# A Mamba-2 and gated DeltaNet block: state-space output by channels in the chunk loop, and a chunk-by-chunk layout for broadcast rows

## Chip, cores and metric

The kernel runs on one core of one Trainium2 chip. The metric is the device time of one execution in microseconds (us); the figure shown for a kernel is the median over its runs.

## What is computed

One layer over a sequence of 1024 tokens of width 1024, in float32: a state-space (SSD) branch and a gated DeltaNet branch in parallel, merged by gates, then a gated conv-MLP and a per-layer embedding. The change touches the state-space recurrence only. With heads `h` of dimension `p` (16 heads of 64 channels), two groups of 8 heads, state size `n` = 128:

```python
seg = a_cum[..., :, None] - a_cum[..., None, :]
lmat = jnp.exp(jnp.where(causal, seg, -jnp.inf))
scores = jnp.einsum('bclgn,bcsgn->bcgls', cc, bc)
y_diag = jnp.einsum('bcgrls,bcsgrp->bclgrp', scores[:, :, :, None] * lmat, xc)
...
y_off = jnp.einsum('bclgn,bcgrpn,bcgrl->bclgrp', cc, prev, jnp.exp(a_cum))
return (y_diag + y_off)          # then + D * x, * silu(z), a norm by group
```

## The kernel before

All five engines run programs written out by hand, each with its own order of work; semaphores tie them together. `after(engine, sem, n)` makes an engine wait until `sem` has been raised n times since the start. DMAs are issued from SP's queue (nearly all loads) and ACT's queue (stores of finished tiles); within a queue a wait holds back all that stands behind it.

The parts, in order of time:

- The head: normalised input, transposed; then tiles of the input projection with their convolutions. On the way ACT (`head_exps`) makes the exponentials of the decay sums and stores the cumulated decay rows of all heads to HBM as `cum_rows` [128 rows, 1024 tokens]. DVE waits for that store (`cum_kept`) ahead of its `raw_op` L3284.
- Pairs of projection tiles by seven products each (L615), with ring buffers `ring_a` that go to the spill area by stores on ACT's queue. A ring slot is rewritten (L624) once its last store has landed.
- Stage A, 8 chunks of 128 tokens: norms and Gram matrices of the DeltaNet branch, set between the k-steps of 16 plain projection tiles (L498, L501, L502). SP loads per chunk `dec_a` twice from `cum_rows` (L1628: 8 rows of 128 tokens, the same rows to all 128 partitions) and `qkv_a` (L1634).
- The chunk loop (`sp_mixer`, `pool_mixer`, `pe_mixer`, `act_mixer`, `dve_mixer`), 8 chunks of 128 tokens, both branches. Between its parts PE runs `gemm(steps[i])`: k-steps of further projection tiles, 12 steps in each of the first four chunks and 8 in the others.
- The rest: branch outputs, MLP, embedding; not touched.

PE's order in a chunk `c` is: products with the DeltaNet state (`ks`, `qs`); `off` (L1128: for each of two groups the C rows of the tokens are stationary and 512 state columns move, so the result has tokens on partitions); gemm; `vn` (needs DVE's `rhs`, L1351); `diag(c, 0)` (L1107), gemm, `diag(c, 1)`; `ds`, `o`; gemm; `st` (L1151); the next chunk's `invert_r`; eight transposes of `ysum` (L1158); gemm; the next chunk's `x_rows_of`, `invert_h`, `scores`; gemm; sums of squares (L1173, needs ACT's L1254 and DVE's `xc`, L1311); `invert_h` (L1088), gemm, `invert_h`; transposes of the DeltaNet output (L1183, need DVE's L1392); gemm.

`diag` takes one head's decay-weighted scores `dec[:, h, :]` as the stationary operand and a pair of heads of `xc` as the moving one, so half of each 128 x 128 result is the wrong head's and DVE (`add_diag`) picks the other half. An f32 matmul shows as two matmul instructions in the trace.

DVE in a chunk: `rhs` (L1348, L1351), `qs` (L1356), `ysum` = off product times exp of the decay sums (L1360), two `add_diag` (L1340), state and output sums, `yssm` += transposed `ysum` (L1383), `yssm` *= `zt` (L1386), next chunk's `xc` (L1311) and inverses, L1392, L1398, L1401, and the scores times decays for the next chunk (`mix_scores`, L1334).

POOL in a chunk: scaling of the states (L1017, L1020), the skip term (L1010), one weight split (L483, L485), then the next chunk's `decays` on `dec` [128 x 2048] (L994, L996), which wait for the load of `dec` (`load_dec`, L923: 16 rows of `cum_rows`, 128 tokens each, to all partitions), and `xcd` (L1003). ACT then takes the exponential (L1237) and, where one is due, empties a projection tile (`mg_evict`, L1219); PE can't begin the next projection tile before that.

SP's order in the loop is `load_g(c)`, `load_qk`, `load_xbc`, `load_bv` for c + 1, a block of weights, then `load_dec`, `load_kd`, `load_mq`, `load_z` for c + 1, then `load_inv(c + 2)`. `load_dec` of the next chunk waits for both `diag` parts of this one.

Of the kernel before, what the change touches and what calls it, by code (L numbers as in the profile page):

```python
# [7 lines left out]
D_MODEL, SEQ = 1024, 1024  # L8
P = 128
# [26 lines left out]
def hybrid_block_kernel(nc, x, p, g_mix_pre, w_in, conv_ssm_w, conv_ssm_b, ssm_dt_bias, ssm_a_log, ssm_d, ssm_norm_g,  # L36
# [7 lines left out]
    def scratch(name, shape):  # L44
        return nc.dram_tensor(name, shape, f32).ap()
# [6 lines left out]
    cum_rows = scratch("cum_rows", [P, SEQ])  # L52
# [12 lines left out]
    def sem(name):  # L65
        return ctx.enter_context(nc.semaphore(name))
# [12 lines left out]
    at = 0  # L79
# [200 lines left out]
    def weights_k(w):  # L280
# [44 lines left out]
    in_xbc, in_qk, in_bv, in_kd, in_mq, in_dec, in_z, in_g, in_nt, in_d = (  # L325
        sem(n) for n in ("in_xbc", "in_qk", "in_bv", "in_kd", "in_mq", "in_dec", "in_z", "in_g", "in_nt", "in_d"))
# [5 lines left out]
    r_done, h_done, xt_done, sc_done, ks_done, qs_done, off_done, vn_done, ds_done, o_done, diag_done, st_done, yt_done, \  # L332
        yssq_done, ot_done = (
            sem(n) for n in ("r_done", "h_done", "xt_done", "sc_done", "ks_done", "qs_done", "off_done", "vn_done", "ds_done",
                             "o_done", "diag_done", "st_done", "yt_done", "yssq_done", "ot_done"))
# [498 lines left out]
    def bank(i, n=1):  # L834
        return ps[:, i:i + n, :].rearrange("p a n -> p (a n)")
# [4 lines left out]
    def wide(ap, n):  # L840
# [48 lines left out]
    def sp_mixer(sp):  # L889
# [71 lines left out]
        load_z(0)  # L961
# [88 lines left out]
    def pe_mixer(pe):  # L1050
# [53 lines left out]
        def diag(c, g):  # L1104
            for i in range(HPG):
                h = g * HPG + i
                last = t.matmul(bank(PB, 2)[:, i * P:(i + 1) * P], dec[:, h, :],  # L1107
                                xc[:, h - h % 2:h - h % 2 + 2, :].rearrange("p h d -> p (h d)"), start=True, stop=True)
            last.then_inc(diag_done, 1)

        def of_group(m, g):
            return m[:, g * HPG:(g + 1) * HPG, :].rearrange("p h d -> p (h d)")

        def main(c, more):
# [12 lines left out]
            for g in range(SSM_GROUPS):  # L1127
                last = t.matmul(bank(PC + g), xbc[:, KD + 2 + g, :], of_group(s_ssm, g), start=True, stop=True)  # L1128
# [24 lines left out]
            after(pe, y_sum, c * 3 + 3)  # L1153
            if more:
                invert_r(c + 1)
            after(pe, o_sum, c * 2 + 2)
            for k in range(KD):
                last = t.transpose(bank(PA, 2)[:, k * P:(k + 1) * P], ysum[:, k * P:(k + 1) * P], ident[:, :])  # L1158
            last.then_inc(yt_done, 1)
            gemm(steps[3])  # L1160
            after(pe, s_ssm_new, c + 1)
            if more:
                x_rows_of(c + 1)
                invert_h(c + 1, 0)
                after(pe, y_mid, c * 2 + 1)
                scores(c + 1)
# [132 lines left out]
    def dve_mixer(dve):  # L1299
# [36 lines left out]
        def add_diag(c, g):  # L1336
            after(dve, diag_done, c * 2 + (g + 1))
            own = bank(PB, 2).rearrange("p (q b d) -> p q b d", q=HPG // 2, b=4)[:, :, 0:4:3, :]
            yg = ysum[:, g * 512:g * 512 + 512].rearrange("p (q b d) -> p q b d", q=HPG // 2, b=2)
            v.tensor_tensor(yg, own, yg, ALU.add).then_inc(y_sum, 1)  # L1340

        def main(c, more):
# [9 lines left out]
            for batch in range(2):  # L1352
# [6 lines left out]
            after(dve, yt_done, c)  # L1359
# [185 lines left out]
    def dve_a(dve):  # L1545
# [10 lines left out]
        dve.wait_ge(cum_kept, 16)  # L1556
# [54 lines left out]
    def sp_a(sp):  # L1611
# [11 lines left out]
        def decays_load(c):  # L1623
            i, tok = c % 2, slice(c * P, c * P + P)
# [35 lines left out]
        sp.wait_ge(cum_kept, 16)  # L1660
# [153 lines left out]
    copied, evicted = later(bs_copied, NCH), later(y_sum, 3 * NCH)  # L1814
# [1268 lines left out]
    def _(act):  # L3083
# [119 lines left out]
    def _(dve):  # L3203
# [108 lines left out]
        dve.wait_ge(cum_kept, 16)  # L3312
# [44 lines left out]
```

## Time and profile before

| | |
|---|---|
| median of 3 runs | 2537.11 us (2535.31 to 2538.26) |
| the profiled execution | 2540.19 us, span 2538.4 us, mean granted clock 0.985 |
| PE busy | 2432.7 us of the span (96%) |
| DVE, ACT, POOL busy | 1533.6, 822.5, 1267.1 us |
| Stage A | about 421 to 705 us |
| the chunk loop | about 769 to 1125 us |

Times in the rows are us from the span's start unless marked ns. A clock of 1.00 in a row is 2.4 GHz and 0.50 is 1.2 GHz. PEld is PE's weight load; a line with SPq or ACTq is the issue of a DMA. The arrow `<-` after a bracket names what the engine waited for.

### The profile page before, as it was taken

Reading aid. Unit: us, or ns where it says so; the run is one execution under the profiler, and the core shown is the slowest. Engines: PE = TensorE matmul, PEld = TensorE weight load, DVE = VectorE, ACT = ScalarE, POOL = GpSimd, SP = SyncE. Lnnn points to the kernel's source line nnn. Section 1 sums busy time; section 2 is a strip of 40 time slices with the busy share of each in tenths; the row PEclk is TensorE's granted clock in tenths of the full one; section 3 lists DMA queues with packets and bytes.
Section 4 is the critical chain, followed back from the end, with each engine's and each line's share of the span. In section 5 each row is a group of like instructions: output and inputs, shape, how many; then the busy total and the mean of one; then the engine's idle time right before and its main releaser. Section 6 shows DMA issues by size and latency. Waiting matters only on the chain. (4 is left out here: it accounts for less than half of the span.)

```text
span 2538.4 us, 29594 instructions
## 1 busy us (share of the span) xinstructions
PE 2432.7 (96%) x11540; PEld 2000.1 (79%) x11540; DVE 1533.6 (60%) x1395; ACT 822.5 (32%) x965; POOL 1267.1 (50%) x687
## 2 busy tenths in 40 slices
PE   7999999899999999989999899999999999999998
PEld 6888887667778877878878678888888878888776
DVE  4987997325765566653243887677677652323575
ACT  5234443445412232331013544334334321000332
POOL 2337887444445455443353266556556543333563
PEclk9999999999999999999999999999999999999999
DMA  6222334688676667644232222222222243122332
GB/s 229 91 84 92 108 120 129 211 266 274 209 220 166 188 173 214 177 144 171 99 134 82 100 78 80 74 93 80 74 93 80 97 177 116 50 83 83 131 106 103
DMA packets 293605, 335.31 MB, mean 132 GB/s; under 512 B 44461, under 2 KB 249594, under 8 KB 289402
## 3 DMA queue, kind: packets, MB, share of 16 engines
q1 hardware_dynamic: 260650, 271.42, 33.9%
q10 hardware_dynamic: 32848, 62.40, 6.7%
q8 instruction: 75, 1.23, 0.2%
q14 instruction: 32, 0.26, 0.0%
HBM read 230.50 MB, written 103.28 MB: 131 GB/s over the span
## 5 line engine op out<-in xcount | busy, mean ns | idle before, releaser
L498 PE MATMUL ps<-act_hi,w_hi 128*128 128x512 f32 x1328 | 535.1, 403 | 19.0 <-ACT ring_b L1219 8.7
L483 POOL TENSOR_SCALAR w_hi<-w_raw 128x1024 fp32r<-128x1024 f32 x123 | 143.9, 1170 | 765.9 <-issue 686.9
L502 PE MATMUL ps<-act_hi,w_lo 128*128 128x512 f32 x1328 | 520.6, 392 | 0.0
L501 PE MATMUL ps<-act_lo,w_hi 128*128 128x512 f32 x1328 | 520.2, 392 | 0.0
L485 POOL TENSOR_TENSOR w_lo<-w_raw,w_hi 128x1024 fp32r<-128x1024 f32 x123 | 333.1, 2708 | 10.3
L498 PEld LDWEIGHTS ps<-act_hi,w_hi 128*128 128x128 f32 x1328 | 251.0, 189 | 78.3 <-ACT ring_b L1219 11.7
L501 PEld LDWEIGHTS ps<-act_lo,w_hi 128*128 128x128 f32 x1328 | 251.5, 189 | 52.9 <-issue 3.3
L502 PEld LDWEIGHTS ps<-act_hi,w_lo 128*128 128x128 f32 x1328 | 251.1, 189 | 53.4
L2050 POOL TENSOR_TENSOR w_lo<-sm,w_hi 128x512 fp32r<-128x512 f32 x120 | 209.0, 1743 | 115.5 <-ACT w_hi L2404 115.5
L2050 POOL TENSOR_TENSOR w_lo<-w_raw,w_hi 128x512 fp32r<-128x512 f32 x90 | 139.2, 1548 | 151.8 <-ACT w_hi L2404 151.8
L2166 PE MATMUL ps<-t,w_hi 128*128 128x512 f32 x480 | 186.8, 389 | 0.2 <-POOL w_lo L2050 0.2
L2167 PE MATMUL ps<-t,w_hi 128*128 128x512 f32 x480 | 186.7, 389 | 0.0
L2168 PE MATMUL ps<-t,w_lo 128*128 128x512 f32 x480 | 186.7, 389 | 0.0
L2166 PE MATMUL ps<-act_hi,w_hi 128*128 128x512 f32 x360 | 140.9, 391 | 3.3 <-DVE ring L2730 2.7
L2168 PE MATMUL ps<-act_hi,w_lo 128*128 128x512 f32 x360 | 140.8, 391 | 0.0
L2167 PE MATMUL ps<-act_lo,w_hi 128*128 128x512 f32 x360 | 140.6, 391 | 0.0
L2813 DVE TENSOR_TENSOR tile<-ps,tile 128x1024 f32<-128x1024 f32 x24 | 29.4, 1224 | 160.8 <-PE ps L502 133.8
L2404 ACT ACTIVATE w_hi<-sm 128x512 fp32r<-128x512 f32 x120 | 75.3, 630 | 134.6 <-PE ps L2168 134.5
L2478 ACT ACTIVATE act_hi<-f_raw 128x1024 fp32r<-128x1024 f32 x32 | 31.2, 1047 | 254.9 <-DMA f_raw<-f_cm 254.9
L579 POOL TENSOR_TENSOR w_lo<-csm,w_hi 128x512 fp32r<-128x512 f32 x48 | 90.9, 1904 | 34.1 <-ACT w_hi L648 33.8
L2166 PEld LDWEIGHTS ps<-t,w_hi 128*128 128x128 f32 x480 | 90.1, 188 | 19.2 <-POOL w_lo L2050 0.6
L2167 PEld LDWEIGHTS ps<-t,w_hi 128*128 128x128 f32 x480 | 90.1, 188 | 18.7
(394 smaller groups left out, 5094.1 us busy)
## 6 DMA issues: line engine op xcount, KB each, us to landing
w_raw<-in_w_in_dram SPq DMA_DIRECT2D x34, 1024.0 KB, 6.7
spill<-ring_a ACTq DMA_DIRECT2D x36, 512.0 KB, 2.6
w_raw<-in_w_ffn_down_dram SPq DMA_DIRECT2D x18, 1024.0 KB, 4.8
w_raw<-in_w_ffn_up_dram SPq DMA_DIRECT2D x16, 1024.0 KB, 5.2
w_raw<-in_w_ffn_gate_dram SPq DMA_DIRECT2D x16, 1024.0 KB, 5.2
f_cm<-ring SPq DMA_DIRECT2D x32, 512.0 KB, 2.6
spill<-ring_b ACTq DMA_DIRECT2D x31, 512.0 KB, 6.9
qkv_a<-spill SPq DMA_DIRECT2D x7, 1536.0 KB, 7.9
```

Source lines behind the costliest of these rows:

```text
L483: nc.gpsimd.tensor_scalar(hi, raw, 1.0, 0.0, ALU.mult, ALU.add).then_inc(split_done, 1)
L485: nc.gpsimd.tensor_tensor(lo, raw, hi.bitcast(f32), ALU.subtract).then_inc(split_done, 1)
L498: first = nc.tensor.matmul(o, wh, mov[0][:, k, c], start=(k == 0), stop=False)
L501: nc.tensor.matmul(o, wh, mov[1][:, k, c], start=False, stop=False)
L502: last = nc.tensor.matmul(o, wl, mov[0][:, k, c], start=False, stop=(k == KD - 1))
L579: nc.gpsimd.tensor_tensor(c_slot(w_lo, j), c_product_in(p, i), c_slot(w_hi, j).bitcast(f32), ALU.subtract).then_inc(c_low[0], 1)
L2050: nc.gpsimd.tensor_tensor(product_slot(w_lo, j), product_in(q, i), product_slot(w_hi, j).bitcast(f32), ALU.subtract).then_inc(w_low[0], 1)
L2166: nc.tensor.matmul(dst, wh[:, k, :], mh[:, k, :], start=(k == 0), stop=False)
L2167: nc.tensor.matmul(dst, wh[:, k, :], ml[:, k, :], start=False, stop=False)
L2168: last = nc.tensor.matmul(dst, wl[:, k, :], mh[:, k, :], start=False, stop=(k == 3))
L2404: a(product_slot(w_hi, j), product_in(q, i), ACT.Copy).then_inc(w_high[0], 1)
L2478: a(hi[:, k, :], raw[:, k, :], ACT.Copy).then_inc(f_hi_done, 1)
```

## The change

- `off` is turned round: for each pair of heads 128 state columns are stationary and the chunk's C rows move, so the result has channels on partitions and tokens along the free axis.
- `diag` is turned round too: a head's 64 columns of `xc` are stationary and its `dec` [128 x 128] moves; even heads write PSUM partitions 0 to 63 and odd heads 64 to 127, so that each pair of heads fills one 128 x 128 result. All 16 heads stand in one block; the gemm that stood between the halves follows it.
- The eight transposes L1158 and their semaphore `yt_done` go. DVE's two `add_diag` become one addition of [128 x 1024]; `yssm` += now reads `ysum` from SBUF.
- The row factors exp(decay sum) now vary along the free axis. They are loaded (`load_e`: two DMAs, 64 partitions each, one for the even and one for the odd heads) from a new HBM array `exp_rows` into `zt`; `load_z` follows once DVE has used them.
- `cum_rows` is laid out chunk by chunk, so that 16 rows of 128 tokens are one run of 8 KB and 8 rows one run of 4 KB. The loads L923 and L1628 take them as such. ACT stores it so, makes one more exponential of [128 x 1024], and stores `exp_rows` by two DMAs; `cum_kept` counts 48.

```diff
-    cum_rows = scratch("cum_rows", [P, SEQ])
+    cum_rows = scratch("cum_rows", [NCH, P, P])
+    exp_rows = scratch("exp_rows", [NCH, 2, KD, P])
...
         def load_dec(c):
-            after(sp, diag_done, c * 2)
-            sp.dma_start(dec[:, :, :], cum_rows[ROW_DT:ROW_DT + SSM_HEADS, tokens(c)].unsqueeze(0).broadcast_to([P, SSM_HEADS, P])
+            after(sp, diag_done, c)
+            sp.dma_start(flat(dec[:, :, :]), cum_rows[c, ROW_DT:ROW_DT + SSM_HEADS, :].rearrange("h t -> (h t)").unsqueeze(0).broadcast_to([P, SSM_HEADS * P])
                          ).then_inc(in_dec, 16)
+        def load_e(c):
+            after(sp, y_mid, c * 2)
+            for i in range(2):
+                rows = exp_rows[c, i].rearrange("k t -> (k t)")
+                sp.dma_start(flat(zt[64 * i:64 * i + 64, :, :]), rows.unsqueeze(0).broadcast_to([64, KD * P])).then_inc(in_e, 16)
         def load_z(c):
-            after(sp, y_mid, c * 2)
+            after(sp, y_sum, c * 2 + 1)
...
             (SP's loop)
                 load_bv(c + 1)
+            load_z(c)
             if c in blocks_at:
...
                 load_mq(c + 1)
-                load_z(c + 1)
+                load_e(c + 1)
...
-        def diag(c, g):
-            for i in range(HPG):
-                h = g * HPG + i
-                last = t.matmul(bank(PB, 2)[:, i * P:(i + 1) * P], dec[:, h, :],
-                                xc[:, h - h % 2:h - h % 2 + 2, :].rearrange("p h d -> p (h d)"), start=True, stop=True)
+        def diag(c):
+            for h in range(SSM_HEADS):
+                d = slice(SSM_HEAD_DIM * (h % 2), SSM_HEAD_DIM * (h % 2) + SSM_HEAD_DIM)
+                last = t.matmul(bank(PB, 2)[d, h // 2 * P:(h // 2 + 1) * P], xc[:, h, :], dec[:, h, :], start=True, stop=True)
...
-            for g in range(SSM_GROUPS):
-                last = t.matmul(bank(PC + g), xbc[:, KD + 2 + g, :], of_group(s_ssm, g), start=True, stop=True)
+            for k in range(KD):
+                last = t.matmul(bank(PC, 2)[:, k * P:(k + 1) * P], s_ssm[:, 2 * k:2 * k + 2, :].rearrange("p h d -> p (h d)"),
+                                xbc[:, KD + 2 + k // 4, :], start=True, stop=True)
...
-            diag(c, 0)
+            diag(c)
             gemm(steps[1])
-            after(pe, y_sum, c * 3 + 2)
-            diag(c, 1)
+            after(pe, y_sum, c * 2 + 1)
...
-            after(pe, o_sum, c * 2 + 2)
-            for k in range(KD):
-                last = t.transpose(bank(PA, 2)[:, k * P:(k + 1) * P], ysum[:, k * P:(k + 1) * P], ident[:, :])
-            last.then_inc(yt_done, 1)
             gemm(steps[3])
...
-                after(pe, y_mid, c * 2 + 1)
+                after(pe, o_sum, c * 2 + 2)
                 scores(c + 1)
...
-            v.tensor_tensor(hd(ysum[:, :]), hd(bank(PC, 2)), wide(head_cols(c, EXP_D, SSM_HEADS), SSM_HEAD_DIM),
-                            ALU.mult).then_inc(y_sum, 1)
-            after(dve, y_sum, c * 3 + 1)
-            add_diag(c, 0)
-            add_diag(c, 1)
+            after(dve, in_e, c * 32 + 32)
+            after(dve, y_mid, c * 2)
+            v.tensor_tensor(hd(ysum[:, :], KD), hd(bank(PC, 2), KD), zt[:, :, :], ALU.mult).then_inc(y_sum, 1)
+            after(dve, diag_done, c + 1)
+            after(dve, y_sum, c * 2 + 1)
+            v.tensor_tensor(ysum[:, :], bank(PB, 2), ysum[:, :], ALU.add).then_inc(y_sum, 1)
...
-            v.tensor_tensor(yssm[:, :, :], hd(bank(PA, 2), 8), yssm[:, :, :], ALU.add).then_inc(y_mid, 1)
+            v.tensor_tensor(yssm[:, :, :], hd(ysum[:, :], KD), yssm[:, :, :], ALU.add).then_inc(y_mid, 1)
...
-                sp.dma_start(dec_a[:, i, at:at + 8, :], cum_rows[row:row + GDN_HEADS, tok].unsqueeze(0).broadcast_to([P, GDN_HEADS, P])
-                             ).then_inc(loaded[i], 16)
+                rows = cum_rows[c, row:row + GDN_HEADS, :].rearrange("h t -> (h t)")
+                sp.dma_start(flat(dec_a[:, i, at:at + 8, :]), rows.unsqueeze(0).broadcast_to([P, GDN_HEADS * P])).then_inc(loaded[i], 16)
...
-            act.dma_start(cum_rows, hrow[:, 1, :]).then_inc(cum_kept, 16)
+            act.dma_start(cum_rows.rearrange("c r t -> r c t"), hrow[:, 1, :].rearrange("r (c t) -> r c t", c=NCH)).then_inc(cum_kept, 16)
+            a(hrow[:, 0, :], hrow[:, 1, :], ACT.Exp).then_inc(tm_act, 1)
+            act.wait_ge(tm_act, 5)
+            for i in range(2):
+                act.dma_start(exp_rows[:, i].rearrange("c k t -> k c t"),
+                              hrow[ROW_DT + i:ROW_DT + SSM_HEADS:2, 0, :].rearrange("k (c t) -> k c t", c=NCH)).then_inc(cum_kept, 16)
...
-        dve.wait_ge(cum_kept, 16)
+        dve.wait_ge(cum_kept, 48)
```

## Rows read from the trace of the kernel before

**Rows 1.** The page, part 1: busy time and share of the span by engine.
```profile
PE 2432.7 (96%) x11540; PEld 2000.1 (79%) x11540; DVE 1533.6 (60%) x1395; ACT 822.5 (32%) x965; POOL 1267.1 (50%) x687
```
**Rows 2.** Waits of PE in stage A, 415 to 720: us in total, times, longest.
```profile
PE ps L1439 <- ACT hrow L1506: 15.2, 3, 9.3
```
**Rows 3.** Timeline of PE, 448 to 486: start, length, work.
```profile
449.47 6.52 PE L1439 MATMUL ps<-hrow,ones 128*128 128x512 f32 x8 [9.31 <-ACT hrow L1506]
...
482.27 3.60 PE L1439 MATMUL ps<-hrow,ones 128*128 128x512 f32 x8
```
**Rows 4.** Timeline of ACT, 427 to 452.
```profile
428.24 0.33 ACTq L633 DMA_DIRECT2D spill<-ring_a  x1
441.50 1.15 ACT L624 ACTIVATE ring_a<-ring_b,par 128x1024 f32<-128x1024 f32 x1 [13.29 <-DMA spill<-ring_a]
```
**Rows 5.** Timeline of SP's queue, 415 to 452.
```profile
421.91 11.68 SPq L1628 DMA_DIRECT2D dec_a<-cum_rows  x4
```
**Rows 6.** DMA issues, 515 to 545: count, KB each, median us to landing.
```profile
qkv_a<-spill SPq DMA_DIRECT2D x1, 1536.0 KB, 17.2
```
**Rows 7.** Windows: busy by engine (PE, PEld, DVE, ACT, POOL), clock, DMA share, GB/s.
```profile
450.00:460.00 10.00, 10.00 (x27) 5.64 (x26) 0.00 (x0) 2.10 (x3) 0.83 (x1) 0.74 0.65 210
540.00:560.00 20.00, 17.23 (x62) 11.84 (x63) 3.67 (x3) 11.36 (x11) 7.72 (x4) 0.83 0.75 254
750.00:760.00 10.00, 9.22 (x46) 7.91 (x47) 2.42 (x3) 1.09 (x2) 2.69 (x3) 0.83 0.31 89
...
1002.00:1006.00 4.00, 3.60 (x9) 2.83 (x10) 3.96 (x4) 0.35 (x1) 4.00 (x3) 0.50 0.85 251
...
1080.00:1084.00 4.00, 4.00 (x17) 3.48 (x16) 4.00 (x1) 0.20 (x1) 4.00 (x2) 0.59 0.00 0
```
**Rows 8.** Waits of PE, 720 to 1110.
```profile
PE ps L1183 <- DVE qs L1392: 9.9, 5, 2.6
PE ps L498 <- ACT ring_b L1219: 6.2, 2, 5.4
PE ps L1070 <- DVE rhs L1351: 4.0, 6, 1.2
PE ps L498 <- POOL w_lo L485: 3.5, 1, 3.5
```
**Rows 9.** Waits of all engines, 700 to 1140.
```profile
POOL dec L994 <- DMA dec<-cum_rows: 120.5, 8, 20.4
...
ACT dec L1237 <- POOL dec L996: 30.0, 7, 9.9
```
**Rows 10.** Line 1398, all its instructions: ns min/median/max.
```profile
L1398 DVE TENSOR_TENSOR yssm<-yssm,sqs x8: 1217/2586/5225, 811.6 to 1118.3; 128x1024 f32<-128x1024 f32 x8
```
**Rows 11.** DMA issues, 780 to 1100.
```profile
dec<-cum_rows SPq DMA_DIRECT2D x7, 1024.0 KB, 17.4
```
**Rows 12.** DMA traffic, 838 to 842, nearly all of it the load of `dec`.
```profile
DMA packets 560, 0.33 MB, mean 83 GB/s; under 512 B 1, under 2 KB 547, under 8 KB 560
```
**Rows 13.** DMA issues, 2484 to 2492 (`g_ple_post`, a 4 KB row, to all partitions).
```profile
fa<-in_g_ple_post_dram SPq DMA_DIRECT2D x1, 512.0 KB, 5.7
```
**Rows 14.** DMA traffic, 2489 to 2490, nearly all of it that load.
```profile
DMA packets 109, 0.39 MB, mean 391 GB/s; under 512 B 12, under 2 KB 14, under 8 KB 109
```
**Rows 15.** Groups of instructions, 770 to 1110: busy us, mean ns, idle before.
```profile
L1107 PE MATMUL ps<-xc,dec 128*128 128x128 f32 x256 | 31.5, 276 | 0.6
...
L1158 PE MATMUL ps<-ident,ysum 128*128 128x128 f32 x64 | 8.3, 273 | 0.0
```
**Rows 16.** Timeline of PE's weight loads, 849 to 854.
```profile
851.40 1.99 PEld L1173 LDWEIGHTS ps<-sqs,ones 128*128 128x128 f32 x16
853.51 0.60 PEld L1088 LDWEIGHTS ps<-xinv,rinv 128*64 128x64 f32 x9
```
**Rows 17.** Timeline of ACT, 152 to 161.
```profile
159.77 1.21 ACT L626 ACTIVATE ring_a<-ps,par 128x1024 f32<-128x1024 f32 x1 [3.14 <-PE ps L502]
```
**Rows 18.** Timeline of DVE, 156 to 184.
```profile
182.77 1.28 DVE L3270 SCALAR_TENSOR_TENSOR ring_a<-ps,par,ring_a 128x1023 f32<-128x1023 f32 x1 [1.91 <-ACT ring_a L626]
```

More of the change, by code:

```diff
@@ L322, in hybrid_block_kernel @@
     blocks_in, sub_step, d_kept, tm_kept = sem("blocks_in"), sem("sub_step"), sem("d_kept"), sem("tm_kept")
-    in_xbc, in_qk, in_bv, in_kd, in_mq, in_dec, in_z, in_g, in_nt, in_d = (
-        sem(n) for n in ("in_xbc", "in_qk", "in_bv", "in_kd", "in_mq", "in_dec", "in_z", "in_g", "in_nt", "in_d"))
+    in_xbc, in_qk, in_bv, in_kd, in_mq, in_dec, in_e, in_z, in_g, in_nt, in_d = (
+        sem(n) for n in ("in_xbc", "in_qk", "in_bv", "in_kd", "in_mq", "in_dec", "in_e", "in_z", "in_g", "in_nt", "in_d"))
     ys_kept, yg_kept = sem("ys_kept"), sem("yg_kept")
@@ L330, in hybrid_block_kernel @@
         sem(n) for n in ("zeroed", "seg_done", "xd_ready", "xcd_ready", "s_ssm_dec", "s_gdn_dec"))
-    r_done, h_done, xt_done, sc_done, ks_done, qs_done, off_done, vn_done, ds_done, o_done, diag_done, st_done, yt_done, \
+    r_done, h_done, xt_done, sc_done, ks_done, qs_done, off_done, vn_done, ds_done, o_done, diag_done, st_done, \
         yssq_done, ot_done = (
             sem(n) for n in ("r_done", "h_done", "xt_done", "sc_done", "ks_done", "qs_done", "off_done", "vn_done", "ds_done",
-                             "o_done", "diag_done", "st_done", "yt_done", "yssq_done", "ot_done"))
+                             "o_done", "diag_done", "st_done", "yssq_done", "ot_done"))
     r_copied, bs_copied, dec_exp, vn_copied, osq_done, ysq_done, orst_done, yrs_done = (
@@ L846, in hybrid_block_kernel @@
     GIVEN = {
-        "sp": (a_in, a_dn[0], a_dn[1], a_dq[0], a_dq[1], in_xbc, in_qk, in_bv, in_kd, in_mq, in_dec, in_z, in_g, in_nt, in_d),
+        "sp": (a_in, a_dn[0], a_dn[1], a_dq[0], a_dq[1], in_xbc, in_qk, in_bv, in_kd, in_mq, in_dec, in_e, in_z, in_g, in_nt, in_d),
         "pool": (a_seg, seg_done, xd_ready, xcd_ready, s_ssm_dec, s_gdn_dec),
         "pe": (a_sum, a_gram, a_vt, a_kt, r_done, h_done, xt_done, sc_done, ks_done, qs_done, off_done, vn_done, ds_done, o_done,
-               diag_done, st_done, yt_done, yssq_done, ot_done),
+               diag_done, st_done, yssq_done, ot_done),
         "act": (a_sq, a_rs, a_exp, kept_qk, kept_bk, kept_d[0], kept_d[1], kept_n[0], kept_n[1],
@@ L960, in sp_mixer @@
         load_mq(0)
-        load_z(0)
+        load_e(0)
         block_load(2)
@@ L1152, in main @@
             last.then_inc(st_done, 1)
-            after(pe, y_sum, c * 3 + 3)
+            after(pe, y_sum, c * 2 + 2)
             if more:
                 invert_r(c + 1)
-            after(pe, o_sum, c * 2 + 2)
-            for k in range(KD):
-                last = t.transpose(bank(PA, 2)[:, k * P:(k + 1) * P], ysum[:, k * P:(k + 1) * P], ident[:, :])
-            last.then_inc(yt_done, 1)
             gemm(steps[3])
@@ L1308, in scale_x @@
             after(dve, xt_done, c + 1)
-            after(dve, diag_done, c * 2)
+            after(dve, diag_done, c)
             after(dve, xcd_ready, c)
@@ L1334, in mix_scores @@
                 v.tensor_tensor(dec[:, g * HPG:(g + 1) * HPG, :], dec[:, g * HPG:(g + 1) * HPG, :], s, ALU.mult).then_inc(m_ready, 1)
[L1336 to L1340, printed above, removed]
         def main(c, more):
@@ L1380, in main @@
             v.reduce_sum(orst[:, :], sqs[:, :, :], mybir.AxisListType.X).then_inc(o_ssq, 1)
-            after(dve, yt_done, c + 1)
+            after(dve, y_sum, c * 2 + 2)
             after(dve, xd_ready, c + 1)
-            v.tensor_tensor(yssm[:, :, :], hd(bank(PA, 2), 8), yssm[:, :, :], ALU.add).then_inc(y_mid, 1)
+            v.tensor_tensor(yssm[:, :, :], hd(ysum[:, :], KD), yssm[:, :, :], ALU.add).then_inc(y_mid, 1)
             after(dve, y_mid, c * 2 + 1)
@@ L1623, in decays_load @@
         def decays_load(c):
-            i, tok = c % 2, slice(c * P, c * P + P)
+            i = c % 2
             after(sp, kept_d[i], 16 * (c // 2))
@@ L1659, in sp_a @@
         sp.wait_ge(tm_kept, len(TM_COLS))
-        sp.wait_ge(cum_kept, 16)
+        sp.wait_ge(cum_kept, 48)
         past(sp, c_prod, PRODUCTS * C_PAIRS)
@@ L1813, in hybrid_block_kernel @@
     prod_done, w_high, w_low, w_sums = (later(sc_done, NCH), later(osq_done, NCH), later(seg_done, 2 * NCH), later(x_scaled, NCH))
-    copied, evicted = later(bs_copied, NCH), later(y_sum, 3 * NCH)
+    copied, evicted = later(bs_copied, NCH), later(y_sum, 2 * NCH)
     t_raw, t_high, t_low = later(o_normed, NCH), later(ysq_done, NCH), later(o_ssq, NCH)
@@ L3311, in _ @@
         dve.wait_ge(tm_kept, len(TM_COLS))
-        dve.wait_ge(cum_kept, 16)
+        dve.wait_ge(cum_kept, 48)
         raw_op(ct3_raw, ct2_raw[:, :, :], part(act_hi, 0, 0), ALU.subtract)
```

1 line of the change is left out of this document (removed).

## The prediction

> **What bounds the kernel.** I read the page first: PE is busy for 96% of the span [rows 1], so what takes time off PE counts, and so does what fills its gaps. There are about 106 us of gaps in all; the next step is to see which of them this change can reach. PE's waits by stage and the windows with their clock show that.
>
> In stage A PE waits 15.2 us for the squares of `qkv_a` (L1506) [rows 2], 9.31 us of it at once at 440, and the products behind it take 6.52 us where the same eight take 3.60 us in the next chunk [rows 3]: they ran at the lower clock (0.74 in that window, 0.83 at 540 [rows 7]). The releaser named is ACT, but ACT stood in its queue at L624, which waited 13.29 us for a store issued at 428.24 [rows 4]. What was under way at the time of that store were four loads of `dec_a`, issued from 421.91 on [rows 5]. At 542 it is `qkv_a` itself that lands 17.2 us after its issue [rows 6], with two `dec_a` loads ahead of it in the queue.
>
> In the loop PE's waits are those for DVE's L1392, for an emptied tile, for `rhs`, and once ahead of the loop for a weight split whose block was late [rows 8]. Behind three of them stands one cause. POOL waits 120.5 us in all for `dec`, and ACT 30.0 us for POOL [rows 9]. So `decays` run late, beside DVE's L1392 and L1398, and L1398 takes 1.22 us at best and 5.2 us at worst [rows 10]; ACT's exponential comes late, so does the tile that it empties behind it (5.4 us of PE's time in chunk 5), and the clock falls to 0.50 for four microseconds after that [rows 7]. `dec` takes 17.4 us to land [rows 11].
>
> Why is that load slow? It moves at 83 GB/s in 512-byte pieces [rows 12], all 128 partitions reading the same 16 short rows. A row of 4 KB to all partitions, `g_ple_post`, lands 512 KB in 5.7 us [rows 13] and moves at 391 GB/s [rows 14]. That is the new shape of `dec_a`, and close to the new shape of `dec` (8 KB).
>
> **The loads, by long rows.** At 391 GB/s `dec` needs 2.7 us for its 1 MB, with some 2 to 4 us around it say 6 in place of 17.4; `dec_a` 1.3 us each and about 4 to land. Stage A: the store of 428.24 then shares the engines with the rest of 2 MB (5.4 us at that rate), lands by about 434, and L624, the taps and L1506 follow 7.5 us earlier or a little more, so PE's stall of 9.31 shrinks to about 0.7: 8.6 us. The products come back to 3.6: 2.9 us. The other two waits of rows 2 (15.2 - 9.3) go: 5.9 us. The clock at 540: 0.17 of 20 us, 3.4 us. Sum 20.8; I take 20. Bounds: nothing if the repeated read itself is the limit, 24 if the lower clock of 450 to 460 is all repaid (0.26 of 10 us less the 2.9 is about nothing, and the 0.7 left and other DMA delays are some 3).
>
> Ahead of the loop the weight block stands behind `dec` in SP's queue: its stall of 3.5 us [rows 8] and the clock loss of 0.17 of 10 us [rows 7], 1.7, give 5.2 us.
>
> In the loop: `dec` is issued earlier as well, since the one `diag` block ends before the gemm. It lands at about the time at which POOL ends its weight split, and `decays` run some 8 to 10 us earlier, clear of L1392 and L1398. Waits 9.9 + 6.2 + 4.0 = 20.1 us [rows 8], clock 0.5 of 4 us at 1002, 2.0, and 0.41 of 4 us at 1080, 1.6 [rows 7]: 23.7 us. Not all of it: with less work on PE the chain from `st` over DVE, ACT and L1173 becomes the later one. DVE's `yssm` sum now reads two SBUF operands, and it and L1386 now fall beside `decays`; at L1398's median of 2.6 in place of 1.22 that makes 2.8 us a chunk, of which the gemm steps around it cover nearly all in the first four chunks and about half in the others. I give back 1 us for each of seven chunks and 3 more for L1183, whose ACT chain stays: 10. Net 13.7, say 14 (0 to 24).
>
> The Trainium skill (SBUF — State Buffer, Who interferes with whom) has it that a DVE operation with two SBUF inputs contends with a GpSimd one that reads SBUF, and one with at most one SBUF input, outside the 2-port modes, does not. By that rule the spread of L1398 is `decays`, and the new `yssm` sum joins the exposed ones; the trace agrees, 1.22 against 5.2. Taken as an exclusive lock for whole instructions it would put each of the two behind a POOL operation; that is the third rival below.
>
> **PE's work.** The transposes L1158 are 8.3 us over eight chunks [rows 15]; in the last chunk nothing of PE's work stands behind to profit, so 7.3. `off` moves the same 2048 columns in pieces of 128 rather than 512, with 16 weight loads for 4, which PE hides behind pieces of 128 in L1107 too (idle 0.6 us for 256) [rows 15]: nothing. `diag` has 256 matmuls of 128 moving columns before and after, busy for 31.5 us [rows 15]. The trace shows no pair of matmuls in two column halves. Below: they follow one another as now, nothing gained. Above: each pair runs at once, half of 31.5, 15.8 us. Going over to the half array costs: between L1173 and L1088 the weight loads stop for 0.12 us [rows 16], and the pipeline has to run empty both ways, some 0.4 us a chunk, 3 us. I take the upper end less that, 12 us, since the halves use other columns, other weights and other PSUM partitions, and nothing in the order of the block (even, odd, even) makes one wait for the other; no row is near enough to prove it.
>
> The Trainium skill (TensorEngine Tiling (Array Packing), Key Properties) says that different tiles can load weights and multiply in parallel, and that changing the tiling mode, not just the tile, drains TensorE. The first would give the 12 us, the second speaks for the 3; only the second has a row here.
>
> **What costs nothing.** DVE's one addition for two, as many elements, on an engine that is busy for 60% [rows 1]; the wait for `load_e` (issued where `load_z` was, a whole half chunk ahead of L1360) and for `load_z` (needed only behind the state sums; SP's wait for L1360 ahead of the weight block and `load_dec` ends before `diag` does). In the head, ACT's extra exponential (about 1 us, as the one in rows 17's line is 1.21) and two issues lie in its wait of 3.14 us [rows 17]. The DVE stands about 3 us longer for `cum_kept` with its raw sums and taps behind it; it has 1.91 us of waiting at 182.77 [rows 18] and more behind, and PE has several tiles in hand: 0, at worst 3.
>
> **Sum.** 20 + 5.2 + 14 + 7.3 + 12 = 58.5 us off 2540.2, the profiled execution's own time: 2481.7. The median of the runs is 3.1 below that execution: 2478.6, so 2479.
>
> **Rivals.**
> - The two column halves don't run at once. For: the trace has no such pair. Then 12 us less, and with a stop of 0.12 us at each of 15 changes of half in a chunk 14 more: 2491 to 2505. Chance 0.27.
> - The broadcast stays slow, since all partitions still read one place. Against: rows 14. Then the 20, 5.2 and 14 go: 2479 + 39 = 2518. Chance 0.07.
> - A new wait replaces the old: `decays` run straight over L1383 and L1386, each at the 5.2 us of rows 10, 8 us a chunk on the chain to L1173. The gemm steps cover about half: 4 us for seven chunks, 28 us: 2507. Chance 0.10.
> - Slower than before: changing halves costs dearly. It must eat 58.5 less the 12, 46.5, and 5 more: 51.5 us over eight chunks, 6.4 a chunk, 0.43 us at each of the 15 changes. A full drain of one f32 matmul (0.276 us long [rows 15]) at each is 4.1 a chunk and does not reach it; with weight loads that can't run ahead it could. Chance 0.04.
> - Loads and PE's work as forecast: 0.50. No measurable change, several of these together: 0.02.
>
> 0.2% (5 us) is about what a measurement of this kernel can tell from no change. Faster than that: 0.50 + 0.27 + 0.07 + 0.10, less a little for their overlap, 0.92; within it 0.03; slower 0.05. The range runs from 2460 (24 in stage A, 24 in the loop, 15.8 in `diag`: 18 less) to 2507, the end of the first and third rivals.
>
> **What would show it.** `dec` landing in 5 to 7 us; POOL's wait at L994 gone from the list; ACT's L624 wait at 441 and PE's at 449 gone, with the clock at 1.00 there; L1398 near 1.22 us; the `diag` block of a chunk at about 2 us rather than 31.5 / 8 = 3.9. It is wrong if `diag` takes 3.9 us or more, if `dec` lands as late as before, or if L1173 or L1070 heads PE's waits in the loop.

## The result, and the profile after

The changed kernel takes 2500.07 us (median of four runs, 2497.19 to 2506.98) against 2537.69: ratio 0.9854, 95% interval 0.983 to 0.9878. The forecast was 2479 (2460 to 2507): faster, and inside the range, but 37.6 us are gone and not 58.5. The profiled execution took 2497.19 us (span 2495.5), 43.0 less than that of before. In the list of busy times PE is busy for 30.8 us less than in [rows 1]:

```profile
PE 2401.9 (96%) x11572; PEld 1981.0 (79%) x11572; DVE 1523.7 (61%) x1387; ACT 821.5 (33%) x966; POOL 1253.3 (50%) x687
```

To see where the time went I cut each profiled span at three starts of PE: the first sums of stage A (L1439 before, L1436 after), the first `ks` product of chunk 0, and that of chunk 7. The first four rows are the two kernels and the two halves of the change (experiments 1 and 2), the others the rest of the experiments.

| kernel | to stage A | stage A to chunk 0 | seven chunks | rest |
|---|---|---|---|---|
| before | 449.5 | 319.4 | 314.4 | 1455.1 |
| after | 449.8 | 310.4 | 280.3 | 1455.0 |
| rows_only | 446.9 | 310.9 | 287.9 | 1453.7 |
| calc_only | 451.6 | 319.2 | 304.7 | 1460.7 |
| halves_apart | 449.2 | 310.8 | 297.1 | 1451.0 |
| early_sums | 446.7 | 311.1 | 288.2 | 1453.4 |
| decays_late | 449.9 | 310.9 | 276.7 | 1454.2 |
| taps_first | 446.2 | 310.8 | 281.0 | 1453.5 |
| copy_first | 450.2 | 302.6 | 281.2 | 1448.5 |
| all_four | 442.3 | 304.5 | 278.8 | 1452.3 |
| rows_three | 442.6 | 302.4 | 289.2 | 1454.9 |
| steps_moved | 442.2 | 302.9 | 275.6 | 1452.0 |

The last column is chunk 7 and all the code behind the loop. Chunk 7 up to its last transposes (L1183) takes 35.1 us before, 31.5 to 34.6 in the others, and 41.6 in calc_only (experiment 2). The code behind it is the same in all, and yet takes 1416.4 to 1422.0 us: a single execution says no more than about 5 us of a long stretch. The kernel before, run again beside the experiments, had medians of 2535.60 (1 to 4), 2534.93 (5 to 7 and all_four) and 2533.73 us (rows_three, steps_moved), so a few us between the medians of two groups can be that. One of the six runs of rows_three took 5971.67 us and is left out of its ratio. Before to after, the loop gave 34.1 us (forecast 14 + 7.3 + 12 = 33.3), and all ahead of it 8.7 (forecast 25.2).

**Ahead of the loop.** PE's waits of 415 to 720, against [rows 2], then those of 720 to 1110, against [rows 8]:

```profile
PE ps L1456 <- DVE hrow L1564: 7.4, 3, 5.4
PE ps L1436 <- ACT hrow L1503: 6.2, 1, 6.2
PE ps L1444 <- ACT hrow L1508: 1.3, 1, 1.3
```
The first and the last of these are not new; the list of before has the last too, and this in place of the first:
```profile
PE ps L1459 <- DVE hrow L1567: 7.5, 3, 5.4
```
From 720 on:
```profile
PE ps L1186 <- DVE qs L1389: 7.5, 6, 1.8
PE ps L1078 <- ACT rinv L1230: 4.5, 1, 4.5
PE ps L1176 <- DVE xc L1314: 3.4, 2, 2.0
PE ps L1176 <- ACT sqs L1257: 2.9, 1, 2.9
PE ps L499 <- ACT ring_b L1222: 2.5, 1, 2.5
```

Of the three waits that made up the 15.2 us of [rows 2] the two smaller ones are gone, and the clock of 540 to 560 is 1.00 where it was 0.83. The longest has become 6.2 from 9.3, and ahead of the loop a new wait of 4.5 us for `rinv` stands where one of 3.5 us for a weight split stood. The timelines of ACT, DVE and POOL around 440, against [rows 4]:

```profile
431.60 0.33 ACTq L634 DMA_DIRECT2D spill<-ring_a  x1
438.16 1.15 ACT L625 ACTIVATE ring_a<-ring_b,par 128x1024 f32<-128x1024 f32 x1 [6.59 <-DMA spill<-ring_a]
...
446.92 1.06 ACT L632 ACTIVATE ring_a<-ring_a 128x1024 f32<-128x1024 f32 x1 [6.66 <-DVE ring_a L731]
```
```profile
439.34 7.55 DVE L731 SCALAR_TENSOR_TENSOR ring_a<-ring_b,par,ring_a 128x1023 f32<-128x1023 f32 x3 [4.44 <-ACT ring_a L625]
```
```profile
439.29 1.90 POOL L1604 TENSOR_TENSOR dec_a<-dec_a,tmc 128x1024 f32<-128x1024 f32 x1
441.26 3.22 POOL L1606 TENSOR_TENSOR dec_a<-dec_a,m_strict 128x1024 f32<-128x1024 f32 x1
```
The same of DVE and POOL before:
```profile
442.68 3.92 DVE L730 SCALAR_TENSOR_TENSOR ring_a<-ring_b,par,ring_a 128x1023 f32<-128x1023 f32 x3 [11.14 <-ACT ring_a L624]
```
```profile
435.90 1.90 POOL L1607 TENSOR_TENSOR dec_a<-dec_a,tmc 128x1024 f32<-128x1024 f32 x1
437.88 2.39 POOL L1609 TENSOR_TENSOR dec_a<-dec_a,m_strict 128x1024 f32<-128x1024 f32 x1
```

ACT waits for the store 6.7 us less than before, as forecast (7.5). But the store is issued 3.4 us later (431.60 for 428.24), and DVE's taps behind it take 7.55 us where they took 3.92, since they now fall on POOL's first work on `dec_a`. Before, POOL was through with it at 440.27, ahead of the taps; now the taps come 3.3 us earlier and POOL 3.4 us later. 3.4 + 3.6 - 6.7 = 0.3: stage A starts where it did. The 3.4 us come from the head. DVE there:

```profile
161.17 2.31 DVE L3286 TENSOR_TENSOR ct_raw<-ct_raw,act_hi 128x2048 f32<-128x2048 f32 x1 [2.98 <-issue]
163.52 4.37 DVE L3286 TENSOR_TENSOR ct_raw<-ct_raw,act_lo 128x2048 f32<-128x2048 f32 x1
```

It waits 2.98 us for the row stores, and the next sum runs into POOL's work (4.37 us, 3.02 before). So do two sums behind it (2.74 and 4.37 us at 171.63 and 174.40, where before they took 2.28 and 2.29), DVE's `csm` comes 5.25 us late (194.77 for 189.52), and at 198.1 PE stands 2.85 us for POOL's w_lo (L580), split from `csm`.

**In the loop.** The groups against [rows 15], and POOL's wait and the landing of `dec` against [rows 9, 11]:

```profile
L1115 PE MATMUL ps<-dec,xc 128*64 128x128 f32 x256 | 15.7, 276 | 0.0
...
L1383 DVE TENSOR_TENSOR yssm<-yssm,zt 128x1024 f32<-128x1024 f32 x8 | 28.1, 3519 | 0.3
...
L1380 DVE TENSOR_TENSOR yssm<-ysum,yssm 128x1024 f32<-128x1024 f32 x8 | 12.2, 1528 | 0.0
```
```profile
POOL dec L1002 <- DMA dec<-cum_rows: 59.5, 7, 12.2
```
```profile
dec<-cum_rows SPq DMA_DIRECT2D x6, 1024.0 KB, 10.0
```

The halves do run at once. The load lands in 10.0 us rather than 17.4 (I had said 6), POOL waits half as long, and old L1398 (now L1395) takes 1.55 us in the mean. The product with `zt` (old L1386) takes 3.5. DVE and POOL in chunk 0 show why:

```profile
785.44 3.62 DVE L1380 TENSOR_TENSOR yssm<-ysum,yssm 128x1024 f32<-128x1024 f32 x1
789.09 5.47 DVE L1383 TENSOR_TENSOR yssm<-yssm,zt 128x1024 f32<-128x1024 f32 x1
```
```profile
784.36 3.61 POOL L1002 TENSOR_TENSOR dec<-dec,tmc 128x2048 f32<-128x2048 f32 x1 [11.32 <-DMA dec<-cum_rows]
788.05 5.43 POOL L1004 TENSOR_TENSOR dec<-dec,m_incl 128x2048 f32<-128x2048 f32 x1
```

POOL's first operation ends at 787.97 and DVE's at 789.06; POOL's second at 793.48 and DVE's at 794.56. Each of DVE's two ends 1.1 us behind POOL's, about its own length of 1.2: it ran only once POOL was done. POOL waits for DVE too: its second operation takes 5.43 us, and 4.55 where DVE is out of the way (experiment 5), 0.9 more, about what DVE's first still had to run when POOL came to its second. That is the third rival's mechanism. PE then stands 2.02 us at 795.80 for DVE's L1314.

### The profile page after: what moved, and what is told of

Its sections match the earlier page's. It is cut to its first block and busy times, and to the rows that moved or that the text cites. A ratio compares the mean times of both kernels' runs of the same rounds, so it can differ in the third digit from the quotient of the medians.

```text
span 2495.5 us, 29692 instructions
## 1 busy us (share of the span) xinstructions
PE 2401.9 (96%) x11572; PEld 1981.0 (79%) x11572; DVE 1523.7 (61%) x1387; ACT 821.5 (33%) x966; POOL 1253.3 (50%) x687
## 5 line engine op out<-in xcount | busy, mean ns | idle before, releaser
L580 POOL TENSOR_TENSOR w_lo<-csm,w_hi 128x512 fp32r<-128x512 f32 x48 | 91.2, 1910 | 30.9 <-ACT w_hi L649 30.9
L2163 PEld LDWEIGHTS ps<-t,w_hi 128*128 128x128 f32 x480 | 90.2, 188 | 19.3 <-POOL w_lo L2047 0.6
```

The source lines that it names most:

```text
L580: nc.gpsimd.tensor_tensor(c_slot(w_lo, j), c_product_in(p, i), c_slot(w_hi, j).bitcast(f32), ALU.subtract).then_inc(c_low[0], 1)
L2163: nc.tensor.matmul(dst, wh[:, k, :], mh[:, k, :], start=(k == 0), stop=False)
```

## The experiments

**1. The layout alone**: before, with only the rows laid chunk by chunk.
```
-            sp.dma_start(dec[:, :, :], cum_rows[ROW_DT:ROW_DT + SSM_HEADS, tokens(c)].unsqueeze(0).broadcast_to([P, SSM_HEADS, P])
+            sp.dma_start(flat(dec[:, :, :]), cum_rows[c, ROW_DT:ROW_DT + SSM_HEADS, :].rearrange("h t -> (h t)").unsqueeze(0).broadcast_to([P, SSM_HEADS * P])
```
(and the same for `dec_a` and for the store.)

> The kernel before with nothing changed but the place of the decay rows (chunk by chunk), so that every load that spreads them reads one long row. Theory L (in the loop the late decays of the next chunk are what the loads cure, and the stages ahead gain little because other waits take over): stage A and what follows up to the first chunk gain 8 to 13 us (the changed kernel has 8.7 there, less 3.3 lost in the head), the seven chunk periods together lose 14 us of their 314.4 (the waits for POOL and for the late product), time about 2512. Theory P (the loop's gain comes from TensorE's own work, the diagonal products and the transposes, and the loads were hidden): the loop stays within 5 us of 314.4 and the time is 2525 or more. In either, the diagonal products take 31.5 us in all.

2500.83 us, ratio 0.9861 (0.9846 to 0.9876): as fast as the whole change. The loop gained 26.5 us, more than either theory said, and in its windows PE is full (columns: stretch, length, busy by engine, clock, DMA share, GB/s):
```profile
801.10:844.40 43.30, 43.24 (x303) 37.70 (x302) 24.81 (x28) 13.08 (x16) 20.85 (x9) 1.00 0.64 198
...
sum 287.90, PE 286.58 PEld 250.25 DVE 175.67 ACT 93.40 POOL 148.98; mean PE 40.94 PEld 35.75 DVE 25.10 ACT 13.34 POOL 21.28
```
The same sum in the changed kernel:
```profile
sum 280.30, PE 270.99 PEld 238.79 DVE 189.17 ACT 93.24 POOL 155.39; mean PE 38.71 PEld 34.11 DVE 27.02 ACT 13.32 POOL 22.20
```
In the changed kernel PE has 15.6 us less to do, but is idle for 9.3 us rather than 1.3. In rows_only `dec` lands in 6.5 us in the median (5.0 to 9.2 by chunk; 9.3 to 11.4 in the changed kernel). No load of `zt` stands ahead of it, but it is issued later too: in chunk 2 it starts 6.3 us behind the load of `bv`, in the changed kernel 1.9 us. Counted from each chunk's first product it lands only 0.1 to 2.6 us earlier, and DVE comes to `yssm` 1.8 us later (27.1 us into chunk 0 for 25.2). So POOL is through the first operation before DVE comes to `yssm`, and the sum reads PSUM. It takes 1.23 us right beside POOL's second operation; only the product with `zt` behind it (2.84) still falls on POOL:
```profile
784.87 1.23 DVE L1383 TENSOR_TENSOR yssm<-ps,yssm 128x1024 f32<-128x1024 f32 x1 [0.31 <-PE ps L1158]
786.12 2.84 DVE L1386 TENSOR_TENSOR yssm<-yssm,zt 128x1024 f32<-128x1024 f32 x1
```
```profile
779.61 3.61 POOL L994 TENSOR_TENSOR dec<-dec,tmc 128x2048 f32<-128x2048 f32 x1 [9.04 <-DMA dec<-cum_rows]
783.30 4.59 POOL L996 TENSOR_TENSOR dec<-dec,m_incl 128x2048 f32<-128x2048 f32 x1
```

**2. The rest alone**: the changed kernel with rows and loads of before.
```
-    cum_rows = scratch("cum_rows", [NCH, P, P])
+    cum_rows = scratch("cum_rows", [P, SEQ])
```

> The changed kernel with the decay rows kept as before (a row of 1024 per head, so that a chunk's load is sixteen or eight short rows); the products by channels, the two halves and the loaded row factors stay. Theory L: the diagonal products take 15.7 us, but the loop keeps the waits for the late decays: it gains 15 to 20 us of 314.4, the head still loses 3.3, nothing is gained ahead of the loop, time about 2522. Theory P: the loop gains 30 us or more even so, time about 2510. A rival to both: the load of decays now may start later (its queue has one more load ahead of it), the two parts need each other, and neither alone gives more than 10 us.

2536.55 us, ratio 1.0004 (0.9993 to 1.0016): nothing. Theories L and P both miss; the rival to both is right that the load comes later still and that this part alone gives nothing, and wrong of the loads, which gave the whole time alone. The loop is 9.7 us shorter in the profile, the head 2.1 longer, chunk 7 6.5 longer. `dec` lands in 20.6 us, and the waits for the emptied tile behind ScalarE's late exponential are 13.2 us in the loop, 6.2 before, with 6.06 us more in chunk 7:
```profile
PE ps L499 <- ACT ring_b L1222: 13.2, 4, 6.4
PE ps L1186 <- DVE qs L1389: 4.4, 3, 3.0
PE ps L1078 <- DVE rhs L1348: 4.4, 5, 1.6
```

**3. The halves one after the other.**
```
-            for h in range(SSM_HEADS):
+            for h in (*range(0, SSM_HEADS, 2), *range(1, SSM_HEADS, 2)):
```

> The changed kernel with the sixteen diagonal products of a chunk in another order: the eight of the even heads (columns 0 to 63) first, then the eight of the odd heads (columns 64 to 127). Theory H (two products run at once only where they follow each other in different column halves): their busy time returns from 15.7 to about 30 us in all, 1.8 us a chunk, and the time goes up by 8 to 15 us to about 2512. Rival (a product over 64 columns is cheaper by itself, whatever stands beside it): busy time stays at 15.7 and the time at 2500.

2510.74 us, ratio 0.9917 (0.9896 to 0.9937): 10.7 us above the changed kernel's median, and 16.8 in the loop of the profile, where PE also waits 9.7 us for DVE's L1314 rather than 3.4. Theory H holds, with a size off: 26.6 us busy, not 30.
```profile
L1115 PE MATMUL ps<-dec,xc 128*64 128x128 f32 x256 | 26.6, 276 | 0.0
...
L1115 PEld LDWEIGHTS ps<-dec,xc 128*64 128x64 f32 x256 | 24.7, 137 | 1.0
```
A weight load of 64 columns takes 137 ns (192 for 128 columns in the kernel before), but little of the way from 31.5 to 26.6 is time gained by it. The busy time counts a tail for each block, and there are two blocks a chunk before and one here. From the start of the block to that of what follows, a chunk's `diag` takes 3.48 to 3.56 us before, 3.26 here and 1.90 in the changed kernel: 0.2 to 0.3 us from narrower weights and one block for two together, and 1.36 from pairs at once.

**4. The head's wait moved** from DVE to ACT, before `sum_high(ct3)`.
```
         dve.wait_ge(tm_kept, len(TM_COLS))
-        dve.wait_ge(cum_kept, 48)
...
             if n == 8:
+                act.wait_ge(cum_kept, 48)
                 sum_high(ct3, ct3_raw, 7)
```

> The changed kernel with the head's wait for the row stores taken from VectorE's queue, where it stood before the sums of ct3 (these overlap only rows that ScalarE's exponentials read), to ScalarE's queue before the rounding of ct3, which is what overlaps the stored rows. Theory W (the wait of 2.98 us at 158.2 and the slower sums behind it cost the head 3.3 us): VectorE's sums start at about 158.1, TensorE's stall at 198 of 2.85 us is gone, the first block load of stage A issues at 415.2 again instead of 418.5, time about 2496.7. Rival (the sums would run beside POOL's splits wherever they start, or ScalarE's new wait holds it): TensorE between 190 and 200 is no busier than 7.2 us and the time stays at 2500.

2496.0 us, ratio 0.9836 (0.9822 to 0.985), in time not to be told from the changed kernel. The profile tells it: the sums start at 158.43, PE has no wait at all from 180 to 415, and the first block load of stage A is issued at 415.54 where it was 418.54. The loop of this execution took 288.2 us with code that took 280.3 before. DVE's two operations on `yssm` fell fully on POOL again in chunk 5, and PE stood for 5.37 us:
```profile
988.60 3.61 POOL L1002 TENSOR_TENSOR dec<-dec,tmc 128x2048 f32<-128x2048 f32 x1 [8.18 <-DMA dec<-cum_rows]
```
```profile
989.04 4.25 DVE L1380 TENSOR_TENSOR yssm<-ysum,yssm 128x1024 f32<-128x1024 f32 x1
993.33 5.44 DVE L1383 TENSOR_TENSOR yssm<-yssm,zt 128x1024 f32<-128x1024 f32 x1
```
```profile
1000.00 2.26 PE L1176 MATMUL ps<-sqs,ones 128*128 128x128 f32 x9 [5.37 <-DVE xc L1314]
```
Less than a microsecond decides. Counted from the first product of chunk 5, DVE's sum begins at 22.5 us in both executions. POOL's first operation began at 22.9 in that of the changed kernel, just behind the sum, and at 22.1 here, just ahead of it: the sum took 4.25 us for 1.22, and the chunk 42.7 for 38.0. Chunk 3 shows the same: POOL at 25.3 there and 24.5 here, the sum at 25.3 in both, the chunk 41.1 and 43.7 us. These two chunks are 7.3 of the 7.9 us between the two loops.

**5. The decays behind the product.**
```
             after(pool, in_dec, c * 16 + 16)
+            after(pool, y_mid, c * 2)
```

> The changed kernel with one wait more: POOL begins the decays of the next chunk only when VectorE has multiplied the output by zt. Theory C (POOL's two operations on dec, when they fall on VectorE's sum and product of yssm, both with operands in SBUF alone, stretch these from 1.2 to 3.6 and 5.5 us, and that is what gives back part of TensorE's saving in the loop): the sum and the product of yssm take 1.2 us each in every chunk, the stalls before the sums of squares (3.4 us in the profile of the changed kernel, 10.2 in that of early_sums) go, the loop takes 271 to 275 us where it took 280.3 and 288.2, time 2491 to 2494. Rival (the decays are needed early, ScalarE's exponential or the next diagonal products then wait): stalls before the diagonal products of 2 to 4 us a chunk, time above 2500.

2492.17 us, ratio 0.9829 (0.9815 to 0.9842). Both operations take 1.2 us in all chunks, the stalls before L1176 are gone, and all that PE waits for in the loop is one line:
```profile
L1384 DVE TENSOR_TENSOR yssm<-yssm,zt 128x1024 f32<-128x1024 f32 x8 | 9.8, 1225 | 0.3
L1381 DVE TENSOR_TENSOR yssm<-ysum,yssm 128x1024 f32<-128x1024 f32 x8 | 9.7, 1216 | 0.0
```
```profile
PE ps L1187 <- DVE qs L1390: 6.1, 7, 1.5
```
The loop takes 276.7 us (271 to 275 expected: I had not counted that wait). No wait for the later decays appears on PE.

**6. The last taps first**, in stage A.
```
             if m == 0:
                 pool.wait_ge(tm_kept, len(TM_COLS))
+                pool.wait_ge(conv_step, 2 * XBC_T + 3 * QKV_T)
```

> The changed kernel with POOL held back from the first decays of stage A until VectorE's last taps are done. Theory T (the taps take 7.55 us, where 3.92 are enough, because POOL's operations on dec_a run beside them, and this is why the earlier landing of the store brought nothing): the taps of 439.3 take 3.9 us, TensorE's stall of 6.21 us before the first sums of stage A falls to about 2.6, the stage starts 3.6 us earlier at a higher granted clock, time about 2495. Rival (POOL's decays and the weights split behind them become the late ones): the stall moves to the weights or to the products of VectorE and the time stays at 2500.

2493.0 us, ratio 0.9833 (0.9818 to 0.9848). The taps take 3.92 us, and PE's stall is 2.87:
```profile
439.43 3.92 DVE L731 SCALAR_TENSOR_TENSOR ring_a<-ring_b,par,ring_a 128x1023 f32<-128x1023 f32 x3 [4.72 <-ACT ring_a L625]
```
```profile
446.22 6.30 PE L1436 MATMUL ps<-hrow,ones 128*128 128x512 f32 x7 [2.87 <-ACT hrow L1503]
```
Stage A starts 3.5 us earlier. The clock did not recover, though PE had stood idle for 2.87 us only: the granted clock is 0.78 in 440 to 450 and 0.88 in the next window, and the eight products take 6.7 us where the changed kernel's took 5.08.

**7. The copies before the stores.**
```
-        d_store(act, 1)
         ready_to_mix(act)
         copy_r(0)
+        d_store(act, 1)
```

> The changed kernel with ScalarE's copies of the first inverse put ahead of its eight stores of the substituted blocks (they wait for VectorE's substitution until 740.9 and take ScalarE's queue until 744.5). Theory S: TensorE's wait of 4.47 us at 745.7 for these copies goes, and the granted clock of 745 to 750 (0.66) stays at 1.00: 4 to 6 us, time about 2495. Rival (VectorE, which is in its substitution until 740.9, or a later store of the blocks is the next to be late): less than 2 us, a wait for xinv or for the second half of the inverse in its place.

2486.81 us, ratio 0.9819 (0.98 to 0.9839). ACT copies at once; before, the same copies stood behind the stores until 745.02, and PE waited (its line in the changed kernel is the second):
```profile
736.65 1.09 ACT L1230 ACTIVATE rinv<-ps 128x512 f32<-128x512 f32 x2 [0.84 <-PE ps L1078]
```
```profile
745.67 3.38 PE L1078 MATMUL ps<-dd,rinv 128*128 128x128 f32 x16 [4.47 <-ACT rinv L1230]
```
Stage A to chunk 0 is 7.9 us shorter: 4.5 of wait, 0.34 of 5 us of clock, and some 2 more that I haven't traced. The medians are 13 us apart, but the kernel before was 2.8 us faster beside this run than beside the changed kernel; by the two ratios (0.9819 and 0.9854) it is 9. In the profile what goes beyond 7.9 lies in the last column of the table; I put it to no cause.

**8 to 10. Together, and the two halves again.** all_four has 4 to 7 at once. rows_three is experiment 1 with 5, 6 and 7. steps_moved is all_four with
```
-            steps = (2, 2, 2, 2, 2, 1, 1) if c < 4 else (2, 1, 1, 1, 1, 1, 1)
+            steps = (2, 2, 2, 2, 1, 2, 1) if c < 4 else (2, 1, 1, 1, 0, 2, 1)
```

> The four changes together: the head's wait moved (early_sums), VectorE's last taps first, the copies before the stores, the late decays. If they add (3.3 + 3.6 + 4.5 + 9), the time is about 2480; if they share their gains through the order of the queues, 2485 to 2492; in any case it is below both kernels, 2500 and 2536.

> The kernel before with the rows laid chunk by chunk (as rows_only), and the three waits of all_four that exist there too: the last taps first, the copies before the stores, the decays after the product with zt. It has neither the products by channels nor the two halves nor the loaded factors. Theory F (in rows_only TensorE has no gap in the loop, 287.9 us with 1.3 us of waits, so only less work for TensorE shortens it): the loop stays at 286 to 289 us, the two waits ahead of it give what they gave in the changed kernel (3.5 and 7.9 us), time 2488 to 2491; the difference to all_four, 10 to 13 us, is what the other part of the change is worth when nothing covers it. Rival (the part is worth nothing, as the equal times of rows_only and the changed kernel say): the time is within 3 us of all_four's 2477.9.

> all_four with one of a chunk's steps of the weight product moved behind the sums of squares, from before them (2, 2, 2, 2, 1, 2, 1 in place of 2, 2, 2, 2, 2, 1, 1, and 0, 2, 1 at the end of the later chunks in place of 1, 1, 1). The sums start 1.4 us earlier, at about 4 us after ScalarE's squares begin, which is still behind them, and TensorE's wait for the normed qs (7.8 us in all, eight times, behind the second logarithm on ScalarE, which waits for the sums) goes: the loop falls from 278.8 to about 272, time about 2471. Rival (the sums then wait for ScalarE's squares by as much): no gain, 2478.

all_four: 2477.87 us, ratio 0.977 (0.9756 to 0.9783), 22.2 us below the changed kernel's median, near the 20.4 forecast for the case that they add. By the stretches of the profile that each was made for, they gave 3.0 + 3.5 + 7.9 + 3.6 = 18.0 us singly and give 14.9 together: most of it adds. rows_three: 2485.95, ratio 0.9807 (0.9795 to 0.982). The intervals are apart, so what experiment 2 found worth nothing is worth 0.4% (8 us between the medians) once nothing covers it; in the profiles the loop is 10.4 us shorter, 278.8 for 289.2. steps_moved: 2472.01, ratio 0.9753 (0.974 to 0.9765), the fastest; its loop is 3.3 us shorter than all_four's, not 7, because in the last three chunks, which have fewer steps, the wait stays:
```profile
PE ps L1187 <- DVE qs L1390: 4.7, 3, 1.8
```

## Why the prediction was right and where it was wrong

**The loop: 33.3 forecast, 34.1 measured, in part by luck.** The loads were to give 23.7 before the giving back; alone they gave 26.5. PE's work was to fall by 19.3; it fell by 15.6. 10 were to be given back; 9.3 - 1.3 = 8.0 were. 26.5 + 15.6 - 8.0 = 34.1. So the terms are each near, but only in this order: with the products first (experiment 2) these give 9.7 and the loads 24.4. And the closeness of the sum is luck: the same loop code took 288.2 us in experiment 4, a gain of 26.2. The 12 for `diag` also counted eight chunks, and the 34.1 are seven. The place of the giving back was half right: the wait for old L1183 stayed, the other part is the collision of experiment 5. PE's work fell by less for two reasons. Busy time counts the modelled tail of each block, which lies over the next: by the starts, a chunk's `diag` went from 1.70 + 1.78 us (two blocks) to 1.90, not by 1.97, and the transposes cost 0.79, not 8.3 / 8. And `off`, which I put at nothing, grew from 1.32 to 1.71 us a chunk, 2.7 us in seven (in chunk 1, from 817.29 to 818.61 before and from 808.25 to 809.96 after). I had read off L1107's idle time that sixteen pieces of 128 columns cost no more than four of 512; its length by the starts, 1.70 to 1.79 us for sixteen pieces, would have shown the price.

**Changing to halves** I put at 0.4 us a chunk. The block ahead of `diag` grew from 1.79 to 1.87 us, the one behind not at all: 0.1.

**"The broadcast moves at 391 GB/s, so 6 us"**: 6.5 where only the layout was changed, 10.0 in the changed kernel, where the load of `zt` now stands ahead of it in the queue and `dec` is issued closer behind the others. I had the order of the queue before me and priced `load_z` at nothing; what it costs by itself no run shows.

**"Head: 0, at worst 3" was wrong.** It cost 3.4 us. The step that failed was to let DVE's slack of 1.91 us at 182.77 [rows 18] stand for the wait's cover. The wait moved the sums into POOL's work, which stretched them, and the chain DVE, POOL, PE had no slack. Experiment 4 returns 3.0.

**"Stage A's first stall shrinks to 0.7" was wrong.** The cause (the store behind the `dec_a` loads) was right, and 6.7 of 7.5 us came. The step that failed: I moved ACT and DVE earlier and did not ask who runs beside DVE then. POOL's decays, which before were through ahead of the taps, now lie beside them and cost them 3.6 us (experiment 6). The late head isn't needed for that: in rows_only, whose head isn't late, the taps take 7.03 us. Of the 20 of stage A, 5.9 of waits, the 3.4 us of clock at 540 and 1.4 of the 2.9 us of slow products came: 10.7.

**"Ahead of the loop 5.2" was wrong.** The weight stall of 3.5 went, and ACT's copies, 4.5 us late behind the stores, were next in line (experiment 7). The clock loss stayed too: 0.66 in 745 to 750. I did not ask what PE would wait for next.

**The signs.** Of those named, the `diag` block came (15.7 / 8 = 1.96 us), and L1398 nearly (1.55 in the mean). `dec` landed in 10.0 us and not 5 to 7, POOL's wait for it halved but did not go (59.5 us), and PE's stall at 449 and its clock stayed in part. None of the three signs of being wrong came in this execution, where the wait for old L1183 heads the loop (5.8 us in the seven chunks); in experiment 4, with the same loop code, it is that of old L1173, 10.2 us.

**The rivals.** The halves run at once (experiment 3), the broadcast did not stay slow (1), changing halves is cheap. The third, `decays` over the two operations on `yssm`, happened. The Trainium skill (SBUF — State Buffer, Who interferes with whom) calls the shared pair an exclusive lock; the ends 1.1 us apart above agree with that, not with a slower sharing. Its price was the error: 28 us forecast, but `dec` lands at the bad moment in some chunks alone, and the steps cover part, so 3.4 us of PE's waits in one execution and 10.2 in another. The same section lets a DVE operation with at most one SBUF input, outside its 2-port modes, run free of POOL; the PSUM sum of experiment 1, 1.23 us beside POOL, agrees.

## What to carry to other kernels

Where a transfer gets faster, list what will now run beside what: here the gains in stage A and in the loop were partly paid back, and the head lost 3.4 us, because DVE and POOL met on SBUF where they had not before; the gain ahead of the loop was paid back because the next wait was as long. Two halves of a change don't add where each hides the other's gain: with the loads late the leaner products gave nothing, and with the loads early and the collisions and the late head left the time was the same with them and without (2500.07 and 2500.83); only after the waits were cleared were they worth 8 us. For work in two column halves, alternate the halves.

## What the hardware showed that I had not expected

- A DVE operation with two SBUF operands that meets a POOL operation on SBUF waits for its end and then takes its own time: 3.62 and 5.47 us for 1.2. POOL's next operation waits for DVE's in turn (5.43 us for 4.55). With a PSUM operand it takes 1.23 us beside the same POOL operation.
- Sixteen f32 products of 64 weight columns took 1.9 us in alternate halves and 3.3 us in an order with one half first, the order being the only difference.
- A load of 1 MB as one long row to all partitions took 6.5 us in the median of seven (5.0 to 9.2), the same bytes as sixteen 512-byte rows 17.4.
- The f32 product `off` took 1.71 us as sixteen instructions that move 128 columns each and 1.32 us as four that move 512, by the starts.
